# Fused Fourier/attention/retention/convolution block with pool and latent-attention layers: output quarters gated from their banks, latent norms spread over a gate quarter, gate quarter four in other banks

## The reference, cut to what matters

```python
def mla_project(h, w_in, q_norm, kv_norm, w_uq, w_ukv, rope):
    proj = h @ w_in
    c_q, c_kv, k_r, gate = jnp.split(proj, [512, 1024, 1088], axis=-1)
    q = (rms_norm(c_q, q_norm) @ w_uq).reshape(B, L, 16, 192)
    kv = (rms_norm(c_kv, kv_norm) @ w_ukv).reshape(B, L, 16, 256)
    ...
    return q_nope, q_rope, k_nope, k_r, v, gate

def mla_branch(...):
    ...
    o_lat = blocked_mla_attend(qn_l, qr_l, kn, kr, v)
    y_lat = (o_lat * jax.nn.silu(g_l)) @ w_out

def second_block(...):
    shift, scale, gate = jnp.split(jax.nn.silu(c) @ ada_w[i] + ada_b[i], 3, axis=-1)
    ...
    x = x + gate[:, None] * rms_norm(y_lat, post_norm[i])
```

## Time and profile before

| | us |
|---|---|
| median of three runs | 2354.02 |
| lowest, highest | 2353.65, 2359.96 |
| the profiled execution | 2357.5 |
| its span, first to last instruction | 2355.6 |
| PE busy | 2207.1 (94%) |
| DVE busy | 1483.0 (63%) |
| ACT busy | 969.0 (41%) |
| POOL busy | 206.3 (9%) |

### The profile page before, as it was taken

The page is one execution under the profiler, slowest core; times in us unless marked ns, Lnnn a source line. Parts: engine busy times, 40 slices in busy tenths (PEclk is TensorE's granted clock), DMA queues, the critical chain, the costliest instruction groups (busy, mean ns, idle before and its releaser), DMA issues.

```text
span 2355.6 us, 33050 instructions
## 1 busy us (share of the span) xinstructions
PE 2207.1 (94%) x13686; PEld 1834.5 (78%) x13686; DVE 1483.0 (63%) x1904; ACT 969.0 (41%) x1340; POOL 206.3 (9%) x392
## 2 busy tenths in 40 slices
PE   5989899998898999998989999999999989999996
PEld 3668778886787877886778888887778979888875
DVE  0445677876754687874685757567786776355544
ACT  2324545453434554554632222223446434344442
POOL 2211010110011010110010101000100110000000
PEclk9989999999998999999999999999999989999998
DMA  9988666768598676668475547454785767322253
GB/s 358 400 250 297 210 234 222 259 225 299 194 301 279 213 277 237 214 217 307 152 251 183 188 135 223 135 186 156 265 279 156 272 208 251 109 63 78 78 188 107
DMA packets 224942, 509.84 MB, mean 216 GB/s; under 512 B 36064, under 2 KB 40288, under 8 KB 222240
## 3 DMA queue, kind: packets, MB, share of 16 engines
q1 hardware_dynamic: 168960, 296.29, 37.4%
q0 software_dynamic: 55696, 211.18, 26.2%
q10 hardware_dynamic: 144, 0.36, 0.0%
HBM read 499.38 MB, written 8.39 MB: 216 GB/s over the span
## 4 chain that ended last, share of the span: by engine, by line
PE 71%; DVE 11%; DMA 9%; ACT 4%; issue 3%; SPq 1%; POOL 0%; DVEq 0%; ACTq 0%; POOLq 0%
PE ps L766 20%; PE ps L767 19%; PE ps L768 19%; DMA w_raw<-in_w_in 4%; DVE ada_acc L2132 3%; DMA ada_raw<-in_ada_w 3%; PE ps L822 3%; DVE wl L2212 1%; DMA w_raw<-in_w_out 1%; PE ps L1427 1%; DVE wl L2219 1%; ACT wh L1529 1%; SPq L598 1%; PE ps L950 1%; PE ps L963 1%
## 5 line engine op out<-in xcount | busy, mean ns | idle before, releaser
L2219 DVE TENSOR_TENSOR wl<-w_raw,wh 128x1024 fp32r<-128x1024 f32 x280 | 335.4, 1222 | 270.8 <-ACT wh L1529 270.0
L1529 ACT ACTIVATE wh<-w_raw 128x1024 fp32r<-128x1024 f32 x280 | 291.7, 1056 | 443.9 <-PE ps L768 281.7
L1582 ACT ACTIVATE wh<-w_raw 128x1024 fp32r<-128x1024 f32 x220 | 230.8, 1058 | 457.4 <-PE ps L768 385.2
L2212 DVE TENSOR_TENSOR wl<-w_raw,wh 128x1024 fp32r<-128x1024 f32 x220 | 266.6, 1221 | 196.7 <-ACT wh L1582 196.3
L766 PE MATMUL ps<-hh,wh 128*128 128x256 f32 x1280 | 374.6, 293 | 11.4 <-DVE hl L2272 7.7
L767 PE MATMUL ps<-hh,wl 128*128 128x256 f32 x1280 | 363.6, 284 | 0.0
L768 PE MATMUL ps<-hl,wh 128*128 128x256 f32 x1280 | 363.1, 284 | 0.0
L2132 DVE SCALAR_TENSOR_TENSOR ada_acc<-ada_raw,cpad,ada_acc 128x1024 f32<-128x1024 f32 x264 | 330.9, 1280 | 25.7 <-DMA ada_raw<-in_ada_w 23.6
L766 PEld LDWEIGHTS ps<-hh,wh 128*128 128x128 f32 x1280 | 245.4, 192 | 35.5 <-issue 20.0
L766 PE MATMUL ps<-wh,act_hl 128*128 128x512 f32 x640 | 257.4, 402 | 9.9 <-DVE wl L2212 9.9
L766 PE MATMUL ps<-act_hl,wh 128*128 128x256 f32 (+1 forms) x736 | 240.6, 327 | 14.6 <-DVE wl L2212 14.5
(11 more groups left out here) (374 smaller groups left out, 3437.1 us busy)
## 6 DMA issues: line engine op xcount, KB each, us to landing
ada_raw<-in_ada_w POOLq DMA_DIRECT2D x272, 512.0 KB, 5.0
w_raw<-in_w_in SPq DMA_DIRECT2D x208, 512.0 KB, 6.3
w_raw<-in_pool_in SPq DMA_DIRECT2D x72, 512.0 KB, 4.5
w_raw<-in_w_out SPq DMA_DIRECT2D x64, 512.0 KB, 5.8
w_raw<-in_mla_in SPq DMA_DIRECT2D x56, 512.0 KB, 5.0
ada_fourth<-in_ada_w POOLq DMA_DIRECT2D x48, 512.0 KB, 6.1
w_raw<-in_pool_out SPq DMA_DIRECT2D x48, 512.0 KB, 5.0
w_raw<-in_mla_out SPq DMA_DIRECT2D x32, 512.0 KB, 4.0
```

What stands on the lines that cost most here:

```text
L1529: act.activation(wh[:, g % RING, :], w_raw[:, g % RING, :], ACT.Copy).then_inc(w_hi, 1)
L1582: act.activation(wh[:, r, :], w_raw[:, r, :], ACT.Copy).then_inc(w_hi, 1)
L2212: dve.tensor_tensor(wl[:, r, :], w_raw[:, r, :], wh[:, r, :].bitcast(F32), ALU.subtract).then_inc(w_lo, 1)
L2219: dve.tensor_tensor(wl[:, g % RING, :], w_raw[:, g % RING, :], wh[:, g % RING, :].bitcast(F32), ALU.subtract).then_inc(w_lo, 1)
```

## The change

- Gate quarter four goes to banks 6 and 7 (`GATE_BANKS`), and ACT's Silu copy of it comes after three of the first pair's four high halves. PE projects the first pair's queries before it waits for that copy; the low half of the rope keys is waited for only before the scores.
- On DVE the norms of both latents are cut into pieces (`mla_norms`) that follow single slots of gate quarter one (`g` 0). ACT's high halves and the second root move with them. The conditioning sums are 0, 6, 8 in `g` 0 to 2 instead of 8, 6, 0; their columns are made before `g` 3, in bank 3. The split of the rope keys moves to `g` 3.
- Output slots 4 and 5 get their high and low halves inside the last pair's step.
- Each output quarter is no longer copied: DVE multiplies it from its banks by the gate row into `ym` (`gated_m`), and ACT squares the banks for the sum. The two take the two tiles in opposite order, one waiting for the other. The root's table is loaded in the second output quarter by a dummy root.
- The end has one operation per tile, `ym * rstd + x`, and SP stores the quarters.

```diff
@@ -180,7 +180,7 @@
                 ("olat", 2, 8, 0), ("olat", 3, 8, 0)]
-MLA_STAGES = [("ckvc", 0, 8, 0), ("krc", 0, 2, 0), ("ckv", 0, 8, 8), ("cq", 0, 8, 8), ("kr", 0, 2, 2), ("g", 0, 8, 8), ("g", 1, 8, 6), ("g", 2, 8, 0),
+MLA_STAGES = [("ckvc", 0, 8, 0), ("krc", 0, 2, 0), ("ckv", 0, 8, 8), ("cq", 0, 8, 8), ("kr", 0, 2, 2), ("g", 0, 8, 0), ("g", 1, 8, 6), ("g", 2, 8, 8),
@@ -458,6 +458,8 @@
         AT_ST = (54, 24)
+        GATE_BANKS = (0, 2, 4, 6)
+        sq_junk = ada_f[:, 512:1536].rearrange("p (t n) -> p t n", t=TT)
@@ -673,6 +675,11 @@
                     g += 1
+            for q in range(4):
+                sp.wait_ge(t_add, 16 + 2 * q + 2)
+                a = slice(q * GRP, (q + 1) * GRP)
+                sp.dma_start(out.rearrange("(t p) n -> p t n", p=P)[:, :, a], x4[:, 0:TT, a]).then_inc(t_x, 16)
+            sp.wait_ge(t_x, 96)
@@ -753,11 +760,7 @@
             pool.dma_start(x4[:, 0:TT, :], save_v).then_inc(x_back, 16)
-            for q in range(4):
-                pool.wait_ge(t_add, 16 + 2 * q + 2)
-                a = slice(q * GRP, (q + 1) * GRP)
-                pool.dma_start(out.rearrange("(t p) n -> p t n", p=P)[:, :, a], x4[:, 0:TT, a]).then_inc(stored, 16)
-            pool.wait_ge(stored, 96)
+            pool.wait_ge(x_back, 16 * DEPTH + 16)
@@ -1305,11 +1308,11 @@
                 elif kind == "g" and i == 2:
-                    pe.wait_ge(m_n, 3)
-                    ada_columns(23)
...
                 elif kind == "g" and i == 3:
-                    pe.wait_ge(m_out, 4)
+                    pe.wait_ge(m_out, 5)
+                    ada_columns(23, 3)
+                    pe.wait_ge(m_n, 3)
@@ -1332,7 +1335,7 @@
                     else:
-                        b0 = 4 if kind == "cq" else (0, 2, 4, 0)[i]
+                        b0 = 4 if kind == "cq" else GATE_BANKS[i]
@@ -1474,16 +1477,17 @@
             r0 = PAIR0 % RING
-            pe.wait_ge(m_out, 6)
-            pe.wait_ge(m_lo, 3)
+            pe.wait_ge(m_out, 4)
+            pe.wait_ge(m_lo, 2)
             pe.wait_ge(ada_read, 24)
+            proj_q(0, r0)
             pe.wait_ge(m_out, 7)
-            proj_q(0, r0)
...
             swap_q(0)
+            pe.wait_ge(m_lo, 3)
@@ -1498,7 +1502,8 @@
                 if q >= 2:
-                    pe.wait_ge(p_y, 6 + q - 1)
+                    pe.wait_ge(p_y, 6 + 2 * (q - 1))
+                    pe.wait_ge(t_mul, 12 + 2 * (q - 1))
@@ -1971,18 +1976,15 @@
                     act.activation(sqb[:, :, 0:SEQ], cqr, ACT.Square).then_inc(m_sq, 1)
+                elif i == 0:
+                    act.activation(krr, ps[:, 6, :], ACT.Copy).then_inc(m_out, 1)
...
                     act.activation(kvh[:, :, :], ckvr, ACT.Copy).then_inc(m_hi, 1)
-                elif kind == "g" and i == 0:
-                    act.activation(krr, ps[:, 6, :], ACT.Copy).then_inc(m_out, 1)
-                    rsqrt_std(m_var, 2, rs_t[:, 0:SEQ], m_std)
-                    act.wait_ge(m_n, 2)
-                    act.activation(cqh[:, :, :], cqr, ACT.Copy).then_inc(m_hi, 1)
...
                         act.wait_ge(stored, 32)
-                    act.activation(om[:, 4 * j:4 * j + 4, :], bank((0, 2, 4, 0)[j], 2).rearrange("p (c t) -> p c t", c=4),
+                    act.activation(om[:, 4 * j:4 * j + 4, :], bank(GATE_BANKS[j], 2).rearrange("p (c t) -> p c t", c=4),
@@ -1993,8 +1995,11 @@
                         mla_extras(kind, i)
-            act.wait_ge(w_used, PAIR0 + RING)
-            mla_extras("g", 4)
+                    if kind == "g" and i == 0 and s == 5:
+                        rsqrt_std(m_var, 2, rs_t[:, 0:SEQ], m_std)
+                    if kind == "g" and i == 0 and s == 7:
+                        act.wait_ge(m_n, 2)
+                        act.activation(cqh[:, :, :], cqr, ACT.Copy).then_inc(m_hi, 1)
@@ -2052,6 +2057,9 @@
                 turned_out(n + 1, 1, 2)
+                if not more:
+                    out_hi(4)
+                    out_hi(5)
@@ -2065,7 +2073,10 @@
-            his_pair(0, (0, 1, 2, 3))
+            his_pair(0, (0, 1, 2))
+            act.wait_ge(w_used, PAIR0 + RING)
+            mla_extras("g", 4)
+            his_pair(0, (3,))
@@ -2097,14 +2108,22 @@
                         act.activation(rowm, bank(0, 4), ACT.Copy).then_inc(t_row, 1)
-                    y_out(2 + q - 1, bank4(4 + 2 * (q % 2), 2), ym[:, :, (q - 1) * GRP:q * GRP], 40, q - 1, TT)
+                        act.activation(st[:, 32:33], st[:, 10:11], ACT.Sqrt)
+                    for t in range(TT):
+                        if t:
+                            act.wait_ge(t_mul, 12 + 2 * (q - 1) + 1)
+                        else:
+                            act.wait_ge(p_y, 6 + 2 * (q - 1))
+                        c = 40 + 4 * t + q - 1
+                        act.activation(sq_junk[:, t, :], ps[:, 4 + 2 * (q % 2) + t, :], ACT.Square, accum_out=st[:, c:c + 1]
+                                       ).then_inc(p_y, 1)
...
                 for s in range(BLK):
-                    if q or s >= 4:
+                    if q or s >= 6:
...
                     g += 1
-                    if q == 0 and s == 4:
+                    if q == 0 and s == 5:
@@ -2683,6 +2702,8 @@
                             extras(kind, i)
+                        if kind == "g":
+                            mla_norms(i, s)
@@ -2757,38 +2778,48 @@
                     dve.tensor_scalar(rs_t, ps[:, 7, :], 1.0 / LORA, EPS, ALU.mult, ALU.add).then_inc(m_var, 1)
+                elif kind == "g" and i == 1:
+                    dve.wait_ge(m_kr, 1)
+                    dve.tensor_copy(krf[:, SEQ:ALL], krr[:, SEQ:ALL])
+                    link(dve.tensor_tensor(krf[:, 0:SEQ], krr[:, 0:SEQ], rope_c, ALU.mult))
+                    link(dve.tensor_tensor(rs_t[:, 0:SEQ], ps[:, 7, 0:SEQ], rope_s, ALU.mult))
+                    dve.tensor_tensor(krf[:, 0:SEQ], krf[:, 0:SEQ], rs_t[:, 0:SEQ], ALU.add).then_inc(m_n, 1)
+                elif kind == "g" and i == 3:
+                    dve.wait_ge(m_n, 3)
+                    link(dve.tensor_copy(krh[:, :], krf[:, :]))
+                    dve.tensor_tensor(krl[:, :], krf[:, :], krh[:, :].bitcast(F32), ALU.subtract).then_inc(m_lo, 1)
+                    ada_result(23, 2, 1, cl("b_ada", 3 * 48 + 40, 8), None, 3)
+            def mla_norms(i, s):
+                if (i, s) == (0, 0):
...
                     link(dve.reciprocal(rs_t, rs_t))
-                    for c in range(NCH):
+                elif i == 0 and s in (1, 2):
+                    for c in range(2 * s - 2, 2 * s):
...
                                                        ALU.mult)
-                    ins.then_inc(m_n, 1)
+                    if s == 2:
+                        ins.then_inc(m_n, 1)
+                elif (i, s) == (0, 4):
...
                     dve.tensor_tensor(kvl[:, :, :], ckvr, kvh[:, :, :].bitcast(F32), ALU.subtract).then_inc(m_lo, 1)
-                elif kind == "g" and i == 0:
+                elif (i, s) == (0, 3):
+                    dve.wait_ge(m_n, 1)
...
                                       ALU.add).then_inc(m_var, 1)
+                elif (i, s) == (0, 6):
...
                     ins.then_inc(m_n, 1)
+                elif (i, s) == (1, 1):
...
                     dve.tensor_tensor(cql[:, :, :], cqr, cqh[:, :, :].bitcast(F32), ALU.subtract).then_inc(m_lo, 1)
-                elif kind == "g" and i == 1:
-                    dve.wait_ge(m_kr, 1)
-                    dve.tensor_copy(krf[:, SEQ:ALL], krr[:, SEQ:ALL])
-                    link(dve.tensor_tensor(krf[:, 0:SEQ], krr[:, 0:SEQ], rope_c, ALU.mult))
-                    link(dve.tensor_tensor(rs_t[:, 0:SEQ], ps[:, 7, 0:SEQ], rope_s, ALU.mult))
-                    dve.tensor_tensor(krf[:, 0:SEQ], krf[:, 0:SEQ], rs_t[:, 0:SEQ], ALU.add).then_inc(m_n, 1)
-                    dve.wait_ge(m_n, 3)
-                    link(dve.tensor_copy(krh[:, :], krf[:, :]))
-                    dve.tensor_tensor(krl[:, :], krf[:, :], krh[:, :].bitcast(F32), ALU.subtract).then_inc(m_lo, 1)
-                elif kind == "g" and i == 2:
-                    ada_result(23, 2, 1, cl("b_ada", 3 * 48 + 40, 8), None)
@@ -2873,6 +2904,9 @@
                 gated_o(p, n, 0)
+                if not more:
+                    lo_of(MLA_OUT0 + 4)
+                    lo_of(MLA_OUT0 + 5)
@@ -2910,13 +2944,27 @@
+            ym = free_.rearrange("p (t n) -> p t n", t=TT)
+            def gated_m(q):
+                dve.wait_ge(t_row, 5)
+                a = slice(q * GRP, (q + 1) * GRP)
+                for t in (1, 0):
+                    if t == 0:
+                        dve.wait_ge(p_y, 6 + 2 * q + 1)
+                    dve.tensor_tensor(ym[:, t, a], ps[:, 4 + 2 * ((q + 1) % 2) + t, :], rowm[:, a], ALU.mult).then_inc(
+                        t_mul, 1)
...
                 for s in range(BLK):
-                    if q or s >= 4:
+                    if q or s >= 6:
...
                     g += 1
```

(17 more changed lines are left out.)

## The result

| | before | after |
|---|---|---|
| runs of the comparison (six each): median, us | 2353.84 (2350.93 to 2359.96) | 2317.38 (2315.48 to 2322.76) |
| ratio after / before, 95% interval | | 0.9843 [0.9826, 0.9860] |
| profiled execution: own time / span, us | 2357.5 / 2355.6 | 2315.48 / 2313.7 |

The kernel is 36.5 us (1.6%) faster. The changed kernel timed a second time, beside other runs of the kernel before, had a median of 2320.33 (ratio 0.9864 [0.9849, 0.9880]), so this measurement repeats to about 3 us.

What follows compares the result with a forecast made beforehand. The prediction took PE's queue, its waits with the low clock behind them, and the tail as the bound. Savings of 15.2 + 5.9 + 3.6 + 8.7 = 33.4 us from the median 2354.0 gave 2320.6 us, range 2317.5 to 2328.

Steps and rivals of the forecast that it cites:

- Part A: Gate projection: latent norms spread over quarter one's slots and conditioning sums moved later let PE run through, 15.2 us saved.
- laid-out queue: Gate quarter one: computed times for DVE and ACT steps, low halves ready 0.9 to 2.7 us before PE wants them.
- allowance of 0.3 for a missed margin: Gate projection: 0.3 us taken off the 15.5 us saving in case one slot's low half comes late.
- Rival 1: Gate quarter one, slots 1, 5, 7: norm chain overruns, 3.7 us together, twice at most, 2324 to 2328; chance 0.17.
- Rival 2: Gate quarter three: conditioning sums still clash there, as a like pattern cost some 5 us before; 2325.5 us, chance 0.12.
- Part C: Gate's end to first key/value matmul: quarter four in banks 6 and 7 frees the query projection, 5.9 us saved.
- Rival 4: First query projection: a high half of pair 0 is still held back, Part C gives nothing; 2326.5 us, chance 0.04.
- Part B: Output projection's start: slots 4 and 5 split in the last pair's step lose 3.9 us of waits, 3.6 us saved.
- Part D: Tail after the last matmul: shorter closing chain, earlier table load and stores from SP, 21.1 to 12.4 us, 8.7 saved.
- Rival 3: Span's end: SP's DRAIN waits for its stores as long as POOL's, +2.7, or +3.8 with slow landing; 2324.4, chance 0.06.
- rival 5: Attention: the clock falls inside it and the kernel gets slower, priced at 41 us, 2361.6 us; chance 0.01.
- 1.0, 0.3 and 0.3: Low end's extra gains: stores landing in 3.2 us (1.0), Part A whole (0.3), output slot 7 in time (0.3).

## Why the prediction was right in its mechanism, and which term was wrong

**Part A (15.2, got 15.4).** The laid-out queue held to 0.1 us at every low half, PE ran through, and the allowance of 0.3 for a missed margin was not needed. The sums in quarter three cost nothing in this profile: no PE wait stands in the gate. Rival 1 did not happen. Rival 2 did not either at its price of 5 us, though in three profiles of eight PE waits 0.2 to 0.8 us at that place. The same pattern of eight sums costs 8.7 us right at the gate's start and 0 to 1.1 us 16 slots later. That this is a matter of lead, as the prediction has it, is a reading: the norms too are gone from DVE's list by then, and no run separates the two.

**Part C (5.9, got 6.0)** came as worked out, though 1.4 us of it hang on how long the clock stayed low in the kernel before. Rival 4 did not happen.

**Part B (3.6, got 3.9).** The one wait of 0.3 before slot 7 came as laid out (0.26); the waits that went are 3.6 us, and the other 0.2 stand in no wait. The low-clock stretch that the two waits can bring was no term of the sum; in the kernel before there was none there.

**Part D (8.7, got 10.0).** Here is the step that failed: "How SP's last store lands no row shows", taken as 4.2 us, between 3.2 and 5.3. It is 2.93, below both ends. Both had been taken from things that were not it: the lower from POOL's store, which is slower by 0.4 us alone and by 1.1 crowded, the upper from loads against a busy read stream. An end from another engine's queue is no lower bound for this one. That is 1.3 us of the 1.9 by which the sum was short; the rest is 0.2 in A, 0.1 in C and 0.3 in B. The 7.7 us to DVE's end were forecast as 7.8. Rival 3, SP's DRAIN waiting for its stores, did not happen: 7 ns.

**Attention** is 215.0 us in both, at clock 1.00; rival 5 did not happen.

**The range** was the second mistake. Its low end took the parts at their best to be 35.0 us (33.4 with 1.0, 0.3 and 0.3), and they were 35.3; 0.27 of the 0.3 is the landing below its lower end. The other 1.5 us down to 2317.5 are "the runs' spread of half a microsecond and more", on three runs of which two agreed to 0.4 and the third lay 5.9 us above. The profiles show the unchanged 1.9 ms ahead of the change to vary by 8 us, and two measurements of one kernel lie 3 us apart. With the sum at 35.3 the forecast would have been 2318.7 (2354.0 less 35.3), and with 3 us for the repeat the low end 2315.7. That the first median fell a tenth outside the range and the second, 2320.33, inside it and close to the forecast is chance of that unchanged stretch.

## What to carry to other kernels

An idle time of PE at the start of a stage can be removed by order alone: put the next slots' splits first and a piece of the long side chain behind each, as long as PE has slots of lead; lay the queues out from durations of the trace, which here gave the times of each step to a tenth of a microsecond. Work that comes in regular portions beside such a chain did less harm once it stood behind it, and it can be pushed out only so far: six sums pushed into the gate cost there what they had cost ahead of it. At a kernel's end, look at which engine issues the last stores: here that was worth 4.2 us, against 0.9 for a table load and 5.6 for the copies and half of the closing operations. And before a range is drawn round such a sum, ask how much the untouched part of the span varies between executions.

## What the runs showed of the hardware

- The closing DRAIN of POOL takes 2.85 us right behind its stores and 2.52 us behind its return of x; SP's takes 0.007 us right behind its stores' last landing and 0.12 behind its last weight load. POOL's stores of 512 KB land later than SP's (3.16 against 2.74 us alone, 3.99 against 2.93 for the last of four at 1.33 us spacing).
- The low clock behind an idle time of the same length differs between executions: after 3.09 us of wait 6.2 us at 0.50 in one and 3 us in another, and after the same two waits at the output's start none in one and 3.4 us in another.
- An unchanged stretch of 1.9 ms took 1907.6 to 1915.6 us over twelve profiles; the largest part of one such difference (5.5 of 6.6 us) was PE waiting for the same loads.
